# Delta rule's channel projections, z and the first gate chunk as three fp32r products, with the weights split on GpSimd

## The reference

```python
proj = xn @ w_in
(sb_q, sb_k, sb_v, g_q, g_k, g_v, g_z, g_b, g_a, gate_sb, gate_gdn) = jnp.split(proj, offs, axis=-1)
o_sb = stick_breaking_attention(heads_sb(sb_q), heads_sb(sb_k), heads_sb(sb_v))
qkv = jax.nn.silu(causal_dwconv(jnp.concatenate([g_q, g_k, g_v], axis=-1), gdn_conv))
...
o_g = gated_delta_rule(cq, ck, cv, beta, g).astype(xn.dtype)
o_g = rmsnorm_2(o_g, gdn_norm_g) * jax.nn.silu(g_z.reshape(B, S, GDN_HEADS, GDN_HEAD_DIM))
merged = jax.nn.sigmoid(gate_sb) * (o_sb @ w_sb_up) + jax.nn.sigmoid(gate_gdn) * (o_g @ w_gdn_up)
return merged @ w_mix_out
```

## Time and profile before

| | |
|---|---|
| median of 3 runs | 1783.69 us (1779.68 to 1785.26) |
| the profiled execution | 1785.51 us, of which the span from first to last instruction is 1783.7 us |
| mean granted PE clock | 0.963 of full speed |
| busy share of the span | PE 91%, PEld 64%, DVE 61%, ACT 32%, POOL 22% |

### The profile page before, as it was taken

The page is one execution under the profiler, slowest core; times in us unless marked ns, Lnnn a source line. Parts: engine busy times, 40 slices in busy tenths (PEclk is TensorE's granted clock), DMA queues, the critical chain, the costliest instruction groups (busy, mean ns, idle before and its releaser), DMA issues.

```text
span 1783.7 us, 22225 instructions
## 1 busy us (share of the span) xinstructions
PE 1627.0 (91%) x7739; PEld 1149.4 (64%) x7739; DVE 1089.5 (61%) x2471; ACT 565.4 (32%) x1123; POOL 393.8 (22%) x313
## 2 busy tenths in 40 slices
PE   7999999999999999999999999888878888888877
PEld 5888999968789999786675595534333434434332
DVE  7557655555476555355645535877677776767765
ACT  2454444334434442333220232222122222212212
POOL 3363100001021000000000002444334444344440
PEclk9999999999999999999999999989888999999888
DMA  6634765515556663234403532999999999999996
GB/s 214 205 104 144 233 199 177 164 63 174 166 176 206 188 184 119 73 144 142 180 31 120 211 125 93 420 420 419 421 420 421 420 422 421 422 420 422 422 421 269
DMA packets 209423, 445.87 MB, mean 250 GB/s; under 512 B 10801, under 2 KB 141265, under 8 KB 174545
## 3 DMA queue, kind: packets, MB, share of 16 engines
q0 software_dynamic: 36864, 268.45, 36.3%
q1 hardware_dynamic: 172496, 176.59, 30.7%
HBM read 440.78 MB, written 4.19 MB: 249 GB/s over the span
## 4 chain that ended last, share of the span: by engine, by line
PE 71%; DMA 16%; DVE 7%; issue 2%; POOL 2%; ACT 2%; SPq 0%; DVEq 0%; ACTq 0%
PE ps L597 33%; PE ps L1514 14%; DMA OT<-in_peer_uv,IX 12%; PE ps L817 7%; PE ps L1311 3%; PE ps L1180 3%; PE ps L1167 3%; PE ps L766 2%; DMA SLOT<-in_peer_uv,IX 2%; DMA SLOT<-in_fox_w_in 2%; DVE SLOT L2970 1%; PE ps L603 1%; POOL SLOT_R L2058 1%; PE ps L675 1%; DVE SLOT_R L2245 1%
## 5 line engine op out<-in xcount | busy, mean ns | idle before, releaser
L1514 PE MATMUL ps<-SLOT,AR 128*128 128x512 f32 x512 | 268.5, 682 | 93.5 <-ACT AR L1982 93.5
L2105 POOL DMA_INDIRECT SLOT<-in_peer_uv,IX x128 | 134.8, 1053 | 774.9 <-DVE IX L2950 536.8
L597 PE MATMUL ps<-ARH 128*128 128x256 f32 (+1 forms) x2120 | 277.5, 286 | 0.0
L597 PEld LDWEIGHTS ps<-ARH 128*128 128x128 f32 x2120 | 266.6, 192 | 3.6 <-issue 0.2
L1514 PEld LDWEIGHTS ps<-SLOT,AR 128*128 128x128 f32 x512 | 110.1, 220 | 245.8 <-issue 132.9
L2970 DVE SCALAR_TENSOR_TENSOR SLOT<-SLOT,V 128x1024 f32<-128x1024 f32 x128 | 153.3, 1224 | 75.3 <-DMA SLOT<-in_peer_uv,IX 73.5
L2245 DVE TENSOR_TENSOR ARH<-SLOT,ARH 128x2048 fp32r<-128x2048 f32 (+1 forms) x88 | 168.3, 1918 | 47.4 <-ACT ARH L1605 31.3
L1514 PE MATMUL ps<-AR 128*128 128x512 f32 x320 | 143.7, 598 | 8.7 <-ACT AR L1982 8.7
L1976 ACT ACTIVATE AR<-AR 128x4 f32<-128x4 f32 (+1 forms) x66 | 13.6, 205 | 376.4 <-DVE SLOT L2970 187.5
L817 PE MATMUL ps<-ARH 128*128 128x512 f32 x528 | 124.5, 391 | 2.0 <-DVE ARH L2245 1.0
L2970 DVE SCALAR_TENSOR_TENSOR AR<-AR,V 128x1024 f32<-128x1024 f32 x80 | 95.6, 1223 | 27.6 <-DMA AR<-in_peer_uv,IX 27.6
(11 more groups left out here) (444 smaller groups left out, 2696.3 us busy)
## 6 DMA issues: line engine op xcount, KB each, us to landing
SLOT<-in_w_gate SPq DMA_DIRECT2D x44, 512.0 KB, 4.0
SLOT<-in_w_up SPq DMA_DIRECT2D x44, 512.0 KB, 5.3
SLOT<-in_w_down SPq DMA_DIRECT2D x44, 512.0 KB, 5.2
SLOT<-in_w_in SPq DMA_DIRECT2D x9, 2048.0 KB, 7.8
SLOT<-in_fox_w_in SPq DMA_DIRECT2D x20, 512.0 KB, 6.7
XT<-in_w_pq_by_head SPq DMA_DIRECT2D x8, 1024.0 KB
SLOT<-in_w_uq_by_pair SPq DMA_DIRECT2D x8, 768.0 KB, 4.6
SLOT<-in_fox_w_o SPq DMA_DIRECT2D x4, 1024.0 KB, 8.5
```

The costliest lines, as they stand in the source:

```text
L597: m = pe.matmul(outp, l, r, start=(n_ == 0), stop=(n_ == len(pairs) - 1))
L1514: m = pe.matmul(ps[:, b, :], DIAG[:, j, :], v_row(j)[:, c * 512:(c + 1) * 512], start=False, stop=closing)
L2105: pool.indirect_dma_start(PAIR[j], None, pairs, bass.IndirectOffsetOnAxis(IX[:, t, j:j + 1], 0)).then_inc(gathered[j], 16)
```

## The change

`channels`, z and gate chunk 0 use three fp32r products. The 8 columns of b and a and the other gate chunks stay float32. XT is split once, into two free stretches of the arena (MIX_X). For the five weights of 1024 x 512, POOL casts each half (128 x 2048) to a high part in a free buffer (XT2 and XS, the arena, the free half of SLOT1) and writes the low part over the weight in its slot: ten casts and ten subtractions of 128 x 2048 in all, beside one cast and two subtractions of 128 x 1024 for XT. PE waits for `mix_split` where it waited for the DMA.

SP loads the first two of these weights ahead of the loop over the rounds' q and k, behind the wait for the kept keys' writes. The third goes to SLOT0 after the last q and k, the fourth (z) to SLOT3, gate chunk 0 to SLOT2, and b and a to WF, a small buffer of their own.

```diff
-        XS = sb("XS", [P, NT, D])
+        XS, XSR = twin("XS", [P, NT, D])
+        MIX_X = (halves(13348, KC, S), halves(15396, KC, S))
+        MIX_FOURS = [view(XT2R[:].rearrange("p a b -> p (a b)"), 4, 512), view(XSR[:].rearrange("p a b -> p (a b)"), 4, 512)]
+        MIX_ARENA = [halves(9252, 4, 512), halves(11300, 4, 512)]
+        MIX_SLOT = [view(SLOTR[1][:, 2048 * q:2048 * q + 2048], 4, 512) for q in range(2)]
+        MIX_WEIGHTS = [(3, MIX_FOURS), (2, MIX_ARENA), (0, MIX_SLOT), (3, MIX_FOURS), (2, MIX_ARENA)]
...
             T.add(used[3])
+            sp.wait_ge(sem("kept"), T.due(sem("kept")))
+            def mixer_weights(s_, c0):
+                fill(s_, (slot(s_, KC, 512), rows(w_in, c0, c0 + 512)))
+
+            mixer_weights(3, 1536)
+            mixer_weights(2, 2048)
             with T.loop("sb", 3) as i:
                 qk(dyn(w_in, i * P + P), dyn(w_in, i * P + (SBW + P)))
-            sp.wait_ge(sem("kept"), T.due(sem("kept")))
-            for n_, s_ in enumerate((3, 2, 3)):
-                fill(s_, (slot(s_, KC, 512), rows(w_in, 1536 + 512 * n_, 2048 + 512 * n_)))
-            fill(2, (slot(2, KC, 512), rows(w_in, 3072, 3584)))
-            sp.wait_ge(used[0], T.due(used[0]))
-            fill(0, (slot(0, KC, 8), rows(w_in, 3584, 3592)))
+            sp.wait_ge(used[1], T.due(used[1]))
+            T.add(used[1])
+            mixer_weights(0, 2560)
+            mixer_weights(3, 3072)
+            sp.dma_start(WF[:, :, 0:8], rows(w_in, 3584, 3592)).then_inc(sem("wf_here"), 16)
...
-            for n_, s_ in enumerate((3, 2, 3, 2)):
-                fill(s_, (slot(s_, KC, 512), rows(w_in, 3592 + 512 * n_, 4104 + 512 * n_)))
+            for n_, s_ in enumerate((2, 3, 2, 3)):
+                mixer_weights(s_, 3592 + 512 * n_)
...
+            def mixer_weight(n_):
+                s_, high = MIX_WEIGHTS[n_]
+                T.add(here[s_], 16)
+                pe.wait_ge(sem("mix_split"), T.next(sem("mix_split")))
+                return lambda h, k: (high[k // 4][:, k % 4, :], low_of(s_, KC, 512)[:, k, :])[h]
-            def channels(s_, g, b):
+            def channels(w, g, b):
                 take(b)
                 for c in range(2):
-                    m = group(ps[:, b, c * S:(c + 1) * S], ((slot(s_, KC, 512)[:, k, (2 * g + c) * P:(2 * g + c + 1) * P], XT[:, k, :])
-                                                             for k in range(KC)))
+                    own = slice((2 * g + c) * P, (2 * g + c + 1) * P)
+                    m = group(ps[:, b, c * S:(c + 1) * S], sum((thirds(lambda h: w(h, k)[:, own], lambda h: MIX_X[h][:, k, :]) for k in range(KC)), []))
...
-            row_tile(2, (6, 7), XT, reader="a")
+            w = mixer_weight(3)
+            for t in range(NT):
+                take(6 + t)
+                group(ps[:, 6 + t, :], mixer_thirds(w, t, range(KC))).then_inc(full["a"][6 + t], 1)
+                T.add(free["a"][6 + t])
+            release(3)
...
+            pool.wait_ge(sem("mix_turned"), 1)
+            pool.tensor_copy(MIX_X[0], XT[:]).then_inc(sem("pool_high"), 1)
+            pool.wait_ge(sem("pool_high"), T.next(sem("pool_high")))
+            for k in (0, KC // 2):
+                ks = slice(k, k + KC // 2)
+                pool.tensor_tensor(MIX_X[1][:, ks, :], XT[:, ks, :], MIX_X[0][:, ks, :].bitcast(F32), ALU.subtract)
...
+            for s, high in MIX_WEIGHTS:
+                pool.wait_ge(here[s], T.next(here[s], 16))
+                for q in range(2):
+                    raw, low = (view(x[s][:], KC, 512)[:, 4 * q:4 * q + 4, :] for x in (SLOT, SLOTR))
+                    pool.tensor_copy(high[q], raw).then_inc(sem("pool_high"), 1)
+                    pool.wait_ge(sem("pool_high"), T.next(sem("pool_high")))
+                    m = pool.tensor_tensor(low, raw, high[q].bitcast(F32), ALU.subtract)
+                m.then_inc(sem("mix_split"), 1)
...
             norm("mix", squared=False)
+            signal("mix_turned")
```

More of the change, by code:

```diff
@@ L153, in twin @@
             return x, nc.alloc_sbuf_tensor_at(name + "_R", shape, F32R, offset=at)
-        ARH = nc.alloc_sbuf_tensor_at("ARH", [P, 17408], F32R, offset=arena_at)
+        ARH = nc.alloc_sbuf_tensor_at("ARH", [P, 17444], F32R, offset=arena_at)
         ps = ctx.enter_context(nc.psum_tensor("ps", [P, 8, 512], F32))
@@ L274, in program @@
         DOT, AV = arena(4080, NT, TOPK), arena(4112, NT, TOPK)
+        ARRIVED = {0: 224, 2: 80, 3: 96}
         DIAG = arena(5600, RING, P)
@@ L1133, in _ @@
             sb_scores(3)
-            pe.wait_ge(here[3], T.next(here[3], 16))
-            channels(3, 0, 0)
+            w = mixer_weight(0)
+            channels(w, 0, 0)
             sb_sums()
             sb_turn()
-            channels(3, 1, 7)
+            channels(w, 1, 7)
             release(3)
@@ L1141, in _ @@
             sb_turn()
-            for n_, s_ in ((1, 2), (2, 3)):
-                pe.wait_ge(here[s_], T.next(here[s_], 16))
+            for n_, freed in ((1, (2,)), (2, (0, 1))):
+                w = mixer_weight(n_)
                 for g in range(2):
-                    channels(s_, g, 2 * n_ + g)
-                release(s_)
-            pe.wait_ge(here[0], T.next(here[0], 16))
+                    channels(w, g, 2 * n_ + g)
+                for s_ in freed:
+                    release(s_)
@@ L1150, in _, with mixer_thirds @@
+            pe.wait_ge(sem("wf_here"), T.next(sem("wf_here"), 16))
             take(0)
             for t in range(NT):
-                m = group(ps[:, 0, 8 * t:8 * t + 8], ((cols(XT, t, k), slot(0, KC, 8)[:, k, :]) for k in range(KC)))
+                m = group(ps[:, 0, 8 * t:8 * t + 8], ((cols(XT, t, k), WF[:, k, 0:8]) for k in range(KC)))
+                first(m)
             m.then_inc(full["v"][0], 1)
             T.add(free["v"][0])
-            release(0)
-            row_tile(2, (6, 7), XT, reader="a")
+            def mixer_thirds(w, t, ks):
+                return sum((thirds(lambda h: cols(MIX_X[h], t, k), lambda h: w(h, k)) for k in ks), [])
@@ L1158, in gate_part @@
+            w = mixer_weight(3)
[4 more added lines that the diff above has]
+            release(3)
+            gate_weight = {}
             def gate_part(n_, b, ks=range(KC)):
                 c, t = n_ // 2, n_ % 2
-                s_ = 3 - c % 2
+                s_ = 2 + c % 2
                 if ks[0] == 0:
-                    if t == 0:
+                    if t == 0 and c == 0:
+                        gate_weight[0] = mixer_weight(4)
+                    elif t == 0:
@@ L1164, in gate_part @@
                         pe.wait_ge(here[s_], T.next(here[s_], 16))
                     take(b)
[L1166 to L1169, removed]
+                if c == 0:
+                    m = group(ps[:, b, :], mixer_thirds(gate_weight[0], t, ks))
+                else:
+                    for k in ks:
+                        m = pe.matmul(ps[:, b, :], cols(XT, t, k), slot(s_, KC, 512)[:, k, :], start=(k == 0), stop=(k == KC - 1))
+                        if k < KC - 1:
+                            first(m)
@@ L2093, in _ @@
                 low_halves(upper(s, at, True), upper(s, at), CK_HIGH[g])
+            pool.wait_ge(sem("mix_turned"), 1)
[4 more added lines that the diff above has]
+                pool.tensor_tensor(MIX_X[1][:, ks, :], XT[:, ks, :], MIX_X[0][:, ks, :].bitcast(F32), ALU.subtract)
+            for s, n in ((0, ARRIVED[0]), (2, ARRIVED[2]), (3, ARRIVED[3])):
+                T.add(here[s], n - T.due(here[s]))
+            for s, high in MIX_WEIGHTS:
[6 more added lines that the diff above has]
+                m.then_inc(sem("mix_split"), 1)
             pairs = a["peer_uv"]
```

## The result

The changed kernel takes 1813.94 us (median, 1810.54 to 1822.04) against 1784.47 us for the kernel before, measured again beside it: a ratio of 1.0173, 95% interval 1.0155 to 1.0191. It is **1.7% slower**. The profiled execution took 1813.29 us against a forecast of 1818.0 for it.

What follows compares the result with a forecast made beforehand. PE was taken to bound the stretch, with DVE held up by POOL's splits. 11.2 + 11.8 + 6.3 - 2.8 + 6.0 = +32.5 us gave 1818.0 for the profiled execution, 1816.2 on the median; range 1794 to 1830.

Steps and rivals of the forecast that it cites:

- Round 1: Stick-breaking round 1: DVE's two-input instructions wait for POOL's splits of weights 0 and 1, +11.2 us, bounds 0 and 14.
- One sign: In round 1, the sums on PE were to have 10 us of idle PE before them.
- Round 4: Stick-breaking round 4: DVE is held by POOL's split of weight 2, +11.8 us, bounds 0 and 13.3.
- PE's savings: Three fp32r matmuls per product save 1.18 us per channels call, 2.8 each in z and gate chunk 0; 12.8 in all.
- the bound: Up to the squares behind the convolution: -8.7 us if all PE's savings come through.
- the 11.6: PE's savings alone: 12.8 us less 1.2 for the first channels call.
- Convolution: DVE's convolution is held by POOL's splits for z and gate chunk 0; squares leave PE idle 15 us, +6.3 net.
- rival 2: Only part of the stalls: 1802 us without round 4's, 1799 without the convolution's; chance 0.17.
- Clock: After PE idles over 10 us at three places, the granted clock falls: 2.0 us each, +6.0, bounds 0 and 10.
- q and k of round 2: Queued behind weight 1, some 3 us later; round 1's stall hides it, without the stall it costs up to 3.
- Rival 1: POOL's splits hide, DVE's wide instructions are not held, only PE's savings are left: 1772 to 1775 us; chance 0.10.
- Rival 3: More loss: POOL's subtraction takes 6.6 us and the clock costs 3.4 each time, 1832 us; chance 0.13.

Runs made afterwards that it cites:

- e9: e7 with the DMAs of round 2's q and k issued ahead of weight 1's; 1778.5 us.
- e10: e9 with the 32 small matmuls of b and a done in two parts, half of them earlier; 1772.6 us.
- e5: The changed kernel with POOL writing zeros over the same bytes instead of splitting the five weights; 1773.2 us.
- e8: The changed kernel with POOL doing only the two casts of each weight, no subtractions; 1775.3 us.
- e1: The changed kernel without the five weights' splits, PE doing the same matmuls on pieces of MIX_X; 1776.2 us.
- e7: The changed kernel with ACT doing the casts and DVE the subtractions, POOL none of the splits; 1779.5 us.
- e6: The changed kernel with POOL starting the third weight's split only after round 4's softplus group on DVE; 1806.7 us.
- e3: The changed kernel with only the first three weights split, z's and gate chunk 0's left out; 1797.0 us.
- e12: e10 once more, with both edits, run and profiled again; 1774.5 us.
- e4: The changed kernel with POOL's casts and subtractions in pieces of 128 x 512 instead of 128 x 2048; 1795.3 us.
- e2: The changed kernel with only z's and gate chunk 0's weights split, the first three left out; 1790.8 us.
- e11: e7 with the small matmuls of b and a in two parts, q and k left behind weight 1; 1777.4 us.

## Why the prediction was right, point by point

Milestones are taken from the values on, the changed kernel against the kernel before.

- **Round 1** was put at +11.2. The second head's last multiplication ended 39.49 behind the values against 30.30: +9.2. POOL had finished weight 0 at 735.16 and not at 736.5, since it began at 722.25 and not at 723, and its subtractions took 4.5 undisturbed and not 4.73. The first absolute value met weight 1's cast, the second its subtraction, the softplus the second subtraction. That was POOL's last one, since its second cast had run in the 2.4 us in which DVE waited for ACT, and the five instructions behind the softplus ran freely, where the working had the addition and the multiplication held as well. One sign was met only in part: PE was to be idle for 10 us before the sums, and it stood for 6.65 there and for 1.61 before q and k.
- **Round 4** was put at +11.8 and measured +10.5 (8.74 from scores to last multiplication before, 19.27 after). The weight landed ahead of the first softplus, as worked out, and the same four POOL instructions held the same kinds. Addition, multiplication and the second softplus were held by just the POOL instructions that the working gave them. It had lengthened both subtractions and the second cast of POOL by DVE's turns between them (5.3, 2.45 and 5.3 us from end to end); they took 4.8, 2.2 and 4.8, and that is the difference.
- **PE's savings** were right. e9, whose rounds cost nothing, begins z 6.0 us early (103.0 behind the values against 109.1): five `channels` calls at 1.18, and next to nothing from the first. e10 reaches the squares 8.6 us early; the bound was 8.7. z's 48 fp32r matmuls take 11.39 us in the changed kernel, 0.237 each: the price from the row of before (0.228) held within 4%, and the Trainium skill's 131 ns (TensorE: Matmul & The Clock Gate, Back-to-back issue gap) is not seen for this type. The rest of the 11.6 was not all to be had, even without POOL: e10's heads are 10.3 us early.
- **Convolution.** POOL came at 818.52, where 818.3 was forecast, and ran its eight instructions in 26.8 us, where 30.1 were forecast: 0.45 us had been added to each for DVE's turn, which POOL doesn't pay. The convolution ended 3.2 us earlier than forecast (857.2 against 837.4 + 23), and the squares waited 11.67 us instead of 15. From b and a to the squares the stretch grew by 9.2 us; this step's forecast, its idle of 15 less z's 2.8, is 12.2. The assumption that rival 2 turned on, that scalar_tensor_tensors of 256 columns are held, is shown by their rows (10.21 and 12.80 us for six) and by e5 against e8.
- **Clock.** Put at 2.0 for each place. Round 1 gave 1.0 (the next scores are +10.2, the multiplication +9.2). Round 4 gave 2.5: from its last multiplication to b and a the stretch shrank by 3.4 where five shorter calls give 5.9. Behind the convolution it was more. Squares to heads grew by 3.1 instead of shrinking by 2.8: 5.9 us, of which 1.6 is a wait for ACT that was not forecast, and 4.3 go with the two windows at 0.50 and one at 0.65. In all 7.8 instead of 6.0.
- **The sum**: 9.2 + 1.0 + 10.5 - 3.4 + 9.2 + 3.1 = +29.6 us in the stretch, against +32.5. The two rounds and the convolution were put 2.0, 1.3 and 3.0 us too high, the clock 1.8 too low, and a wait of 1.6 for ACT was missing. So 3.4 us of the 6.3 too much were cancelled by luck. Over the whole profiled execution the difference is +27.8: the values start 0.4 us earlier, and what follows the heads is 1.4 us shorter.
- **q and k of round 2** waited 1.61 us for their DMA in place of about 3, and round 1's stall hid it, as said. Without the stall it costs 1.5, in e1 and e7.
- **The rivals.** Rival 1 didn't happen, but it gave the time of the matmuls alone: 1772 to 1775, where e1 has 1776.2, e5 1773.2 and e10 1772.6. Rival 2 had 1802 for no stall in round 4; e6, which makes just that, has 1806.7, since the stall moves on in part. It had 1799 for no stall in the convolution; e3 has 1797.0. Rival 3's 6.6 us for a subtraction was far off: the longest here took 4.70.

What stays open: the lower medians of e10 and e12, and why the clock falls behind b and a in some of these kernels only.

## What to carry to other kernels

Before moving work to an idle POOL, find DVE's instructions that run beside it: here each that has two SBUF inputs waited for the end of the POOL instruction beside it, where that one read SBUF. So multiply POOL's instruction length by the number of turns on the path, and not the total of POOL's work. If POOL has to do it, cut its instructions short (e4 gave back 18.5 of 29.6 us for a loop bound); but where ACT and DVE have gaps, they do the same work (2.3 us against 4.5 for a subtraction, 1.9 against 1.9 for a cast) and hold nobody. And when a stall goes, look at what comes up next: here a DMA order (1.5 us) and a run of small matmuls (1.6 us of z in e9) hid under it.

## What the runs showed of the hardware that was not expected

- The granted clock falls without PE being idle. In e1, e2 and e4 to e9 it read 0.50 to 0.71 in a window of 4 us at or behind the end of 3.6 to 4.1 us of 8-column matmuls, and z took 12.9 to 14.0 us; with the same 32 matmuls in two runs of 1.85 us (e10, e11, e12) it stayed at 1.00 and z took 11.4. The changed kernel itself and e3 have the 32 in one run and a z of 11.4 and 11.3, and the kernel before has them too with the clock at 1.00 behind them, so such a run doesn't always do it.
- A memset of POOL holds a tensor_scalar of DVE (2.42 and 3.10 us for two instead of 0.62), but not a scalar_tensor_tensor or tensor_tensor.
- POOL pays little for sharing with short DVE instructions. In this stretch, where DVE's take 0.35 to 0.56 us alone, its cast of 128 x 2048 is 1.89 us alone and 1.90 to 2.23 beside DVE, its subtraction 4.5 and 4.5 to 4.7. It is no privilege of POOL: at 526 us in the kernel before, beside DVE subtractions of 128 x 1024 and more, its pair of subtractions of 128 x 1024 took 7.68 us instead of 4.75, and DVE's took 3.4.
